# Row sums of two norms (attention and linear attention) in two fp32r passes, half a weight unit later

## The reference, cut to what matters

```python
def rmsnorm(x, g):
    xf = x.astype(jnp.float32)
    y = xf * lax.rsqrt(jnp.mean(xf * xf, axis=-1, keepdims=True) + EPS)
    return (y * g).astype(x.dtype)
```

## Time and profile before

| | |
|---|---|
| median of 3 runs | 2086.0 us |
| profiled execution, its own time | 2085.84 us |
| its span | 2084.0 us |
| TensorE matmul busy | 2074.8 us (100%), x10112 |
| weight load busy | 1731.5 us (83%) |
| VectorE, ScalarE, GpSimd busy | 968.3, 499.3, 1513.2 us |
| granted TensorE clock | 1.0 of full speed |

### The profile page before, as it was taken

How to read it: one execution, slowest core, us unless ns; L and a number is a source line. 1 busy time by engine, 2 the same in 40 slices (tenths; PEclk the granted TensorE clock), 3 DMA queues, 4 the chain that set the end, 5 groups by cost and what they waited for, 6 DMA issues and landing times.

```text
span 2084.0 us, 28662 instructions
## 1 busy us (share of the span) xinstructions
PE 2074.8 (100%) x10112; PEld 1731.5 (83%) x10112; DVE 968.3 (46%) x1459; ACT 499.3 (24%) x999; POOL 1513.2 (73%) x1607
## 2 busy tenths in 40 slices
PE   9999999999999999999999999999999999999999
PEld 7888888888788878888888888889888888888887
DVE  6565655521456665755542166436753243222100
ACT  2002111100266674211100044222353122111000
POOL 7788888867864547888877775546545788777675
PEclk9999999999999999999999999999999999999999
DMA  5323333323343223333323332223222333333233
GB/s 158 100 86 102 99 100 92 101 84 93 107 107 87 82 82 86 91 100 91 101 85 94 98 92 81 61 71 102 72 64 70 90 107 96 97 94 101 86 91 96
DMA packets 368163, 192.45 MB, mean 92 GB/s; under 512 B 8672, under 2 KB 364608, under 8 KB 368080
## 3 DMA queue, kind: packets, MB, share of 16 engines
q1 hardware_dynamic: 365280, 186.52, 31.0%
q10 hardware_dynamic: 2800, 4.83, 0.8%
HBM read 189.19 MB, written 2.13 MB: 92 GB/s over the span
## 4 chain that ended last, share of the span: by engine, by line
PE 95%; DVE 2%; ACT 1%; issue 1%; DMA 0%; SPq 0%; DVEq 0%; ACTq 0%
PE PS L571 22%; PE PS L573 22%; PE PS L572 22%; PE PS L882 3%; PE PS L884 3%; PE PS L883 3%; PE PS L898 2%; PE PS L899 2%; PE PS L900 2%; PE PS L730 1%; PE PS L732 1%; PE PS L731 1%; PE PS L1081 1%; PE PS L693 1%; PE PS L758 1%; PE PS L760 1%
## 5 line engine op out<-in xcount | busy, mean ns | idle before, releaser
L554 POOL TENSOR_TENSOR RING<-RAW,RING 128x512 fp32r<-128x512 f32 x704 | 975.8, 1386 | 58.7
L551 POOL TENSOR_SCALAR RING<-RAW 128x512 fp32r<-128x512 f32 x704 | 517.9, 736 | 344.7 <-PE PS L884 90.5
L571 PE MATMUL PS<-XH,RING 128*128 128x512 f32 x1296 | 504.8, 389 | 0.0
L573 PE MATMUL PS<-XH,RING 128*128 128x512 f32 x1296 | 504.2, 389 | 0.0
L572 PE MATMUL PS<-XL,RING 128*128 128x512 f32 x1296 | 504.2, 389 | 0.0
L571 PEld LDWEIGHTS PS<-XH,RING 128*128 128x128 f32 x1296 | 243.3, 188 | 51.5 <-issue 1.1
L572 PEld LDWEIGHTS PS<-XL,RING 128*128 128x128 f32 x1296 | 243.3, 188 | 50.7 <-issue 0.2
L573 PEld LDWEIGHTS PS<-XH,RING 128*128 128x128 f32 x1296 | 243.3, 188 | 50.4
L571 PE MATMUL PS<-HH,RING 128*128 128x512 f32 x528 | 205.6, 389 | 0.0
L573 PE MATMUL PS<-HH,RING 128*128 128x512 f32 x528 | 205.4, 389 | 0.0
L572 PE MATMUL PS<-HL,RING 128*128 128x512 f32 x528 | 205.4, 389 | 0.0
(11 more groups left out here) (342 smaller groups left out, 3404.7 us busy)
## 6 DMA issues: line engine op xcount, KB each, us to landing
RAW<-in_ffn_w_up SPq DMA_DIRECT2D x88, 512.0 KB, 3.7
RAW<-in_w_in SPq DMA_DIRECT2D x52, 512.0 KB, 3.6
RAW<-in_w_ffn_in SPq DMA_DIRECT2D x44, 512.0 KB, 3.7
RAW<-in_ffn_w_down SPq DMA_DIRECT2D x32, 512.0 KB, 4.1
RAW<-in_a_w_in SPq DMA_DIRECT2D x24, 512.0 KB, 3.7
RAW<-in_b_w_qg SPq DMA_DIRECT2D x16, 512.0 KB, 3.7
RAW<-in_w_kvf SPq DMA_DIRECT2D x16, 512.0 KB, 3.9
RAW<-in_w_ffn_out SPq DMA_DIRECT2D x16, 512.0 KB, 3.8
```

What stands on the lines that cost most here:

```text
L551: hi = pool.tensor_scalar(WH[s][:, k0_:k1, :], RAW[r][:, k0_:k1, :], 1.0, 1.0, ALU.mult, ALU.mult)
L554: lo = pool.tensor_tensor(WL[s][:, k0_:k1, :], RAW[r][:, k0_:k1, :], WH[s][:, k0_:k1, :].bitcast(F32), ALU.subtract)
L571: pe.matmul(o, WH[s][:, k, :], xh[:, k0 + k, :], start=first and k == 0, stop=False)
L573: mm = pe.matmul(o, WL[s][:, k, :], xh[:, k0 + k, :], start=False, stop=last and k == nk - 1)
```

## The change

Norms 1 and 3 take the split way too. VectorE makes ACCH and ACCL behind every residual that has a norm after it, and the semaphore values count two steps for each norm. In attention the sums go between the halves of unit 1. In GLA they go behind piece 1, and the transposes, `fold` and both sets of gate tiles each go one piece further on. `row_sums` is gone.

```diff
-            def row_sums(n):
-
-                pe.wait_ge(sem("acc"), tiles(n) + KT)
-                pe.matmul(PS[:, 7, :], ONE[:, :], W[1][:, 0:S], start=True, stop=True).then_inc(sem("nsum"), 1)
-
             def row_sums_split(n):
 
                 one = ONE[:, :].bitcast(F32R)
-                pe.wait_ge(sem("acc_split"), n + 2)
+                pe.wait_ge(sem("acc_split"), 2 * n + 2)
...
                 unit(p, 0, 0, 0, XH, XL, ready=(sem("xld"), 1, scaled(1)))
-                row_sums(1)
-                unit(p, 0, 1, 1, XH, XL)
+                half_unit(p, 1, 0, 1, XH, XL)
+                row_sums_split(1)
+                half_unit(p, 1, 1, 1, XH, XL)
                 unit(p, 0, 2, 2, XH, XL)
...
             def gla():
                 narrow_products(3, 3)
                 gla_dense(0, 0)
-                row_sums(3)
-                for n in range(1, 3):
-                    gla_dense(0, n)
+                gla_dense(0, 1)
+                row_sums_split(3)
+                gla_dense(0, 2)
+                gla_dense(0, 3)
                 pe.wait_ge(sem("narrow"), 4)
                 for t in range(TB):
                     tr = pe.transpose(PS[:, 5, t * P:(t + 1) * P], W[0][:, t * P:(t + 1) * P], IDF[:, :])
                 tr.then_inc(sem("scale_t"), 1)
-                gla_dense(0, 3)
+                gla_dense(0, 4)
                 fold(LRT[:, :], 4)
-                gla_dense(0, 4)
+                gla_dense(0, 5)
                 pe.wait_ge(sem("up_loaded"), 128)
                 gate_tiles(0, 4)
-                gla_dense(0, 5)
                 gla_dense(0, 6)
+                gla_dense(0, 7)
                 gate_tiles(4, 8)
-                for n in range(7, 10):
+                for n in range(8, 10):
                     gla_dense(0, n)
...
-                if gains and n % 2 == 0:
+                if gains:
                     dve.wait_ge(sem("acc"), tiles(n) + KT)
                     dve.tensor_copy(ACCH[:, :], W[1][:, 0:S]).then_inc(sem("acc_split"), 1)
-                    dve.wait_ge(sem("acc_split"), n + 1)
+                    dve.wait_ge(sem("acc_split"), 2 * n + 1)
```

## The result

The changed kernel takes 2094.46 us (median of 7 runs, 2092.37 to 2095.34) against 2085.97 us before (median of 7, 2085.63 to 2086.29): ratio 1.0039, 95% interval 1.0029 to 1.0048. It is 8.5 us slower. The forecast was 2091.3 us in a range of 2088.5 to 2093.3: the sign was right, the size too small, and the time lies outside the range. Two things stand out before any row is read: the loss is more than the waits that I had added up, and the runs now spread over 3.0 us where they spread over 0.7.

The account below looks back on a forecast made before the run. TensorE's work and few waits were taken as the bound. Attention's 2.1 us and GLA's 3.4 us, savings counted in, made 5.5 us on 2085.84: 2091.3 us, range 2088.5 to 2093.3.

Parts of the forecast that it names:

- Bound, and the saving of 0.40 us a norm: TensorE's order bounds the kernel; two fp32r passes (0.47 us) replace a plain sum (0.87 us), 0.8 us for both norms.
- The norm 2.34 us later: In both layers, sums behind 12 more matmuls (2.73 us) make the norm start 2.34 us later.
- Attention, the wait at the first head sum: First head sum already waits for HSQL, 0.06 us after its end; attention loses 2.1 us, bounds 1.3 and 3.2.
- GLA, two waits: Piece 4 waits 0.6 us for q, piece 8 waits 2.5 us for v; GLA loses 3.4 us, bounds 2.4 and 4.3.
- GpSimd's collision: In GLA, GpSimd meets the first scan, which may cost 1.0 us ahead of v; GLA near 3.4 and not 2.7.
- The piece that covered the chain had gone ahead of the tiles: In GLA, the value block covering VectorE's chain to v now precedes the gate tiles, so piece 8 waits 2.5 us.
- The casts at nothing: VectorE's cast and subtraction, 2.24 us, cost nothing: its idle time ahead of the mean, 2.15 and 2.17 us, covers them.
- a delay of about 1 us: If the sums stood at their old place, the casts' cover would be gone and they would delay the norm this much.
- The sum: Attention 2.1 plus GLA 3.4 is 5.5 us, savings counted in, on 2085.84 us: 2091.3 us.
- later waits stay as they are: Behind both places TensorE, VectorE and ScalarE are equally late, so no later wait changes; weights only get more time.
- GpSimd's collisions pile up: Rival: some four VectorE steps behind GLA's gate tiles take 1.0 us more each, turned keys late; 2094.3 us, chance 0.08.

Follow-up runs that it names:

- the filled kernel: The changed kernel plus 11 unread fp32r matmuls ahead of the first head sum and 12 ahead of piece 8: 2092.10 us, ratio 1.0030.

## Why the prediction was right and wrong

- **Bound, and the saving of 0.40 us a norm**: right (0.47 us for the two passes, 0.44 and 0.39 us saved).
- **The norm 2.34 us later**: right, 2.31 in attention; in GLA the mean came at 1213.04 against 1207.34, less the 3.33 us by which TensorE was late already, 2.37.
- **Attention, the wait at the first head sum**: right in place and size (2.14 net, 2.1 taken). The scan became shorter (1.51) and HSQL longer (1.31), as bounded.
- **GLA, two waits**: right, 0.54 for 0.6, and 2.85 for 2.5 with GpSimd's collision on top. The collision was taken at 0.7 us and up to 1.0; ahead of v it cost 0.3 (the scan 1.51 for 1.22), so piece 8 lost 3.16 us for the 3.4 taken. The piece that covered the chain had gone ahead of the tiles, as the working says.
- **The casts at nothing**: wrong at the new place. Their cover was read on VectorE alone. Without them the chain behind was 1.4 us shorter there and the kernel 2.2 us faster; by GpSimd's rows they had kept it from its backlog, though that is not tested by itself. At the old place, where the prediction gave the norm a delay of about 1 us, it was 1.12 in GLA and 0.2 in attention.
- **The sum**: this is the step that failed. Each wait was costed at its length, and the work behind it at the pace of 0.228 us a matmul; what the wait does to that pace was put at nothing. Behind both waits the granted clock fell to 0.50, which cost 1.35 and 2.86 us in the profiled execution, and 2.4 us between the medians of the unfilled and the filled kernel. Filled, the same kernel is at 2092.1 us, within the range and 0.8 from the forecast. The profile before shows a mean granted clock of 1.0, and I took the clock for a constant. A second, smaller term failed too: "later waits stay as they are". In the filled kernel the product of v with the keys waits where it did not, some 0.6 us. No rival had the clock: "GpSimd's collisions pile up" had the size, 2094.3, by another cause, and that it stands so near the 2094.46 measured is chance.

The Trainium skill (TensorE: Matmul & The Clock Gate, What's actually happening) has a clock gate that takes TensorE to half speed after idleness. The trace agrees with the direction: 0.54 and 0.50 granted behind 2.66 and 2.85 us without a matmul. It belonged into the prediction as a rival: it would have made each long wait cost more than its length.

What stays open is what decides whether, and for how long, the clock falls. It does not take the whole wait: in GLA the last matmul ended at 1234.36, and from 1236.00 to 1237.20, still within the wait, the mean granted clock is 0.63 already. Waits of 2.84 and 2.85 us at the same place were followed by about 3 and 6 us of half speed, and in the profiled execution of the kernel with plain sums at the new places 2.85 us were followed by none:

```profile
1235.35 0.47 PE L883 MATMUL PS<-XH,RING 128*128 128x512 f32 x1 [2.85 <-ACT VG L1512]
1235.65 0.40 PE L884 MATMUL PS<-XL,RING 128*128 128x512 f32 x1
1235.88 0.39 PE L885 MATMUL PS<-XH,RING 128*128 128x512 f32 x1
```

## What to carry to other kernels

A step may move later only as far as the slack of the tightest operand behind it, and in an order written by hand the slack is worth following to the first place that waits already: here 0.06 us stood against a move of 2.3. Where a change leaves TensorE idle as long as here (2.7 and 2.9 us), count the wait, and as its upper end some microseconds of the work behind it at half speed (1.35 and 2.86 us more here); where the wait can't be removed, a few matmuls into a free bank, even for half of it, give that part back. Before an engine's idle time is taken as free cover for added work, look at what its neighbour does in that time: here GpSimd ran its backlog off in VectorE's idle time.

## What the hardware showed that was not expected

- TensorE ran at 0.50 of its clock for 3 to 6 us behind waits of 2.66 to 2.85 us, in some executions; behind 1.50 and 1.25 us it did not, and behind one of 2.85 us neither. The sign of it in the times is the spread: 3.0 us over 7 runs with the unfilled waits, 0.3 us with filled ones.
- The same VectorE instructions take different times beside GpSimd's, by the moment at which they meet: the scan 2.20, 1.51 and 1.23 us in these kernels. At the new place the chain from the mean to HSQL took 28.4 us with 2.5 us of casts ahead of it and 27.0 without, at the old place 28.37 and 28.55, though not one instruction of that chain was changed.
